# Another placement of the tiles in SBUF: the split weights 48 bytes past a multiple of 16 KB

## What is computed

```
h = rms_norm(x, ln_pre_g)
proj = einsum('bsd,de->bse', h, w_in)            # 2048 x 18432
...                                              # recurrence, attention, gates
y = einsum('bsd,de->bse', merged, w_o)
x = x + rms_norm(y, ln_post_g)
for l in range(2):
    h = rmsnorm(x, g_pre_2[l])
    u = h @ w_in_2[l]                            # 2048 x 16192
    ...                                          # three attention branches
    x = x + (gated sum of branch @ w_branch_2[l, n]) @ w_out_2[l]
```

## The kernel before

| tile | bytes | offset | over a multiple of 16 KB |
|---|---|---|---|
| raw | 16384 | 16512 | 128 |
| hl | 32768 | 32896 | 128 |
| hT, uT | 32768 each | 65664, 98432 | 128 |
| xres, mix, gat | 16384 each | 131200, 147584, 163968 | 128 |
| corr | 4096 | 180352 | 128 |
| cst, tab | 1536, 7168 | 184448, 185984 | 4224, 5760 |
| work | 32256 | 194752 | 14528 |

## Time and profile before

### The profile page before, as it was taken

One profiled execution on the slowest core, in us unless ns is written; L12 is line 12 of the kernel. 1 busy time (PEld: TensorE's weight loads), 2 busy tenths in 40 slices (PEclk: granted clock), 3 DMA queues, 4 the chain that ended last, 5 costly groups with the idle time before them and its releaser, 6 DMA issues.

```text
span 3154.9 us, 52176 instructions
## 1 busy us (share of the span) xinstructions
PE 3134.1 (99%) x18230; PEld 2741.8 (87%) x18230; DVE 2130.5 (68%) x2741; ACT 1733.0 (55%) x2291; POOL 0.2 (0%) x4
## 2 busy tenths in 40 slices
PE   9999999999999999999999999999999999999999
PEld 7888888888888788888888888888888888888888
DVE  7677575666667687766666555777776666655575
ACT  5685444444445556656555555645665656555563
POOL 0000000000000000000000000000000000000000
PEclk9999999999999999999999999999999999999999
DMA  7656655555556555565556655566556565665555
GB/s 230 194 168 200 198 187 166 183 177 172 181 167 208 178 168 163 156 198 173 174 171 192 184 181 182 181 198 186 158 157 202 170 179 167 192 189 180 178 185 175
DMA packets 569809, 571.67 MB, mean 181 GB/s; under 512 B 26352, under 2 KB 565488, under 8 KB 569712
## 3 DMA queue, kind: packets, MB, share of 16 engines
q1 hardware_dynamic: 569712, 570.42, 58.9%
HBM read 568.25 MB, written 2.10 MB: 181 GB/s over the span
## 4 chain that ended last, share of the span: by engine, by line
PE 97%; DVE 1%; ACT 1%; DMA 0%; SPq 0%; issue 0%; ACTq 0%; DVEq 0%
PE pg L537 91%; PE pa L771 1%; PE pa L788 1%; PE pa L537 1%; PE pa L778 1%; PE pa L747 1%; PE pa L789 1%; DVE hl L1276 0%; PE pa L704 0%; DMA raw<-w_o 0%; PE pa L878 0%; DMA raw<-w_in 0%; ACT hl L933 0%; SPq L456 0%; DVE uT L1357 0%
## 5 line engine op out<-in xcount | busy, mean ns | idle before, releaser
L537 PE MATMUL pg<-hT,hl 128*128 128x512 f32 x11456 | 2030.6, 337 | 1.1 <-DVE hl L1276 1.1
L537 PEld LDWEIGHTS pg<-hT,hl 128*128 128x128 f32 x11456 | 1750.9, 188 | 261.1 <-DVE hl L1276 4.2
L1276 DVE TENSOR_TENSOR hl<-raw,hl 128x1024 fp32r<-128x1024 f32 (+1 forms) x1071 | 1256.0, 1209 | 314.5 <-ACT hl L933 306.8
L933 ACT ACTIVATE hl<-raw 128x1024 fp32r<-128x1024 f32 (+1 forms) x1071 | 1084.0, 1044 | 313.1 <-PE pg L537 293.8
L537 PE MATMUL pg<-uT,hl 128*128 128x256 f32 (+1 forms) x3712 | 639.1, 333 | 15.9 <-DVE uT L1357 7.5
L537 PEld LDWEIGHTS pg<-uT,hl 128*128 128x128 f32 x3712 | 558.4, 190 | 92.2 <-issue 14.2
L941 ACT ACTIVATE corr<-pg 128x512 f32<-128x512 f32 x286 | 170.3, 596 | 843.0 <-PE pg L537 843.0
L537 PE MATMUL pg<-hl,hT 128*128 128x256 f32 (+1 forms) x1792 | 317.9, 336 | 0.0
L1283 DVE TENSOR_TENSOR work<-pg,corr 128x512 f32<-128x512 f32 (+1 forms) x154 | 105.8, 687 | 303.7 <-ACT corr L941 303.5
L537 PEld LDWEIGHTS pg<-hl,hT 128*128 128x128 f32 x1792 | 274.9, 188 | 40.7
L1283 DVE TENSOR_TENSOR gat<-pg,corr 128x512 f32 (+1 forms) x71 | 48.9, 689 | 139.4 <-ACT corr L941 139.4
(11 more groups left out here) (191 smaller groups left out, 1369.2 us busy)
## 6 DMA issues: line engine op xcount, KB each, us to landing
raw<-w_in SPq DMA_DIRECT2D x791, 512.0 KB, 4.7
raw<-w_br SPq DMA_DIRECT2D x96, 512.0 KB, 4.3
raw<-w_out SPq DMA_DIRECT2D x64, 512.0 KB, 4.7
raw<-w_rnn SPq DMA_DIRECT2D x32, 512.0 KB, 4.8
raw<-w_o SPq DMA_DIRECT2D x32, 512.0 KB, 5.0
raw<-w_att SPq DMA_DIRECT2D x16, 512.0 KB, 4.4
raw<-w_uq SPq DMA_DIRECT2D x16, 384.0 KB, 4.0
tab<-tabs SPq DMA_DIRECT2D x5, 896.0 KB, 7.2
```

The source lines that it names most:

```text
L537: return nc.tensor.matmul(out, lhsT, rhs, start=start, stop=stop, skip_group_check=True)
L933: nc.scalar.activation(hl4[:, j % 2, 0, a:a + n], raw[:, bass.ds(j % 2 * UC + a, n)], ACT.Copy)\
L1276: tt(hl4[:, j % 2, 1, a:a + n], raw[:, bass.ds(j % 2 * UC + a, n)], hl4[:, j % 2, 0, a:a + n].bitcast(F32), ALU.subtract).then_inc(lo_done, 1)
```

## The change

Only the order in which SBUF tiles are allocated and two constants change. The small tiles come first, then an unused tile `pad` of 464 columns (1856 bytes) fills up to offset 32768. `raw` starts there. `hl` gets 12 more columns (48 bytes) at its front, which `hl4` skips. The program's instructions and their order are the same on every engine; only addresses differ.

```
--- before.py
+++ after.py
@@ -56,6 +56,8 @@
 ROT_HALF = {"1": 16, "B": 8}
 
 T_C, T_S, T_R, T_M, N_TAB = 0, 256, 512, 640, 640 + 1152
+PAD = 464
+SHIFT = 12
 T_RG = T_M + 384
 
 def events(text):
@@ -200,8 +202,16 @@
         def sem(name):
             return ctx.enter_context(nc.semaphore(name))
 
+        corr = sb("corr", 2 * 512)
+        cst = sb("cst", 3 * P)
+        tab = sb("tab", N_TAB)
+        v1 = sb("v1", N_V1)
+        v2 = sb("v2", N_V2)
+        sm = sb("sm", 200)
+
+        sb("pad", PAD)
         raw = sb("raw", 2 * UC)
-        hl = sb("hl", 4 * UC, F32R)
+        hl = sb("hl", SHIFT + 4 * UC, F32R)
         hT = sb("hT", NT * 512, F32R)
         uT = sb("uT", NT * 512, F32R)
         xres = sb("xres", NT * S)
@@ -209,18 +219,12 @@
             sq_a = [mix_r[:, 5 * S * h:5 * S * h + 5 * S].rearrange("p (t n) -> p t n", n=S) for h in range(2)]
         mix = sb("mix", NT * S)
         gat = sb("gat", NT * S)
-        corr = sb("corr", 2 * 512)
-        cst = sb("cst", 3 * P)
-        tab = sb("tab", N_TAB)
-        v1 = sb("v1", N_V1)
-        v2 = sb("v2", N_V2)
-        sm = sb("sm", 200)
         work = sb("work", 31 * 256 + 128)
         pg = ctx.enter_context(nc.psum_tensor("pg", [P, 4 * 512], F32))
         pa = ctx.enter_context(nc.psum_tensor("pa", [P, 4 * 512], F32))
 
 
-        hl4 = hl[:, :].rearrange("p (s h n) -> p s h n", s=2, h=2)
+        hl4 = hl[:, SHIFT:].rearrange("p (s h n) -> p s h n", s=2, h=2)
         h3 = hT[:, :].rearrange("p (t n) -> p t n", n=512)
         u3 = uT[:, :].rearrange("p (t n) -> p t n", n=512)
         x3 = xres[:, :].rearrange("p (t n) -> p t n", n=S)
```

## The result

The changed kernel takes 3196.45 us (median of four, 3195.83 to 3196.71) where the one before takes 3156.33 us. The ratio is 1.0124, with a 95% interval of 1.0112 to 1.0137: 40 us slower. The forecast was 3156 us with 3112 to 3186 us as its range, so the time lies 10 us above the range, on the side to which 0.17 of the chances were given.

A forecast was written before the change was run, and what follows sets the result against it. TensorE's matmul rate was taken to bound the kernel. The span of 3154.9 us, four terms of 0 and 1.4 us from span to median gave 3156.3 us, with a range of 3112 to 3186 us.

The forecast's parts named there:

- What bounds the kernel: TensorE, busy 99% of the span with 17 us of waits; so its matmul rate decides the time.
- It is a fixed 13.3 ns per matmul: Each wide or narrow TensorE matmul costs 32 cycles beyond its columns, a fixed sum and not a share.
- the first term of the sum: TensorE's weight load (hl) against its moving operand (hT or uT): interval -176 us to an unknown loss, taken as 0.
- the constancy of the earlier trace: Time per matmul agreed within 0.25 ns across chunks and long stretches, so 0 was taken for TensorE's reads.
- the sign for fixedness: The excess per matmul was the same 13.3 ns in mixed stretches and in narrow ones alone, at 120.0 ns each.
- The slower one: hl's weight blocks cover nine 64-byte pieces instead of eight: four cycles more per matmul, 28 us, 3184 us; chance 0.17.
- The faster one: The 32 cycles are a collision of TensorE's two reads, ended wholly (2980 us) or a quarter (3112 us); chance 0.22.
- The third: hl lands 16, not 48, bytes from hT and uT, possibly missing any effect; same forecast, no chance of its own.
- The small terms: VectorE's split (1 us either side), ScalarE's copy, float32 matmuls and transfers into raw (0.6 us), all taken as 0.
- an unknown loss: Open upper end of the TensorE term, as no distance under 512 bytes was in the trace; 0.04 beyond 28 us.

The follow-up runs named there:

- g2: Kernel before with hl as before, hT 32 bytes further from it and uT 112 further, modulo 128; 3165.39 us.
- e3: Kernel before with hl, hT and uT moved together by 48 bytes, distances kept; 3157.59 us.
- e1: First half of the change alone on the kernel before: small tiles first and the 1856-byte pad, no 48 bytes; 3174.67 us.
- f4: As e1 but with a pad 128 bytes longer, so large tiles lie 128 over a multiple of 16 KB; 3167.92 us.
- f3: Kernel before with hl moved by 48 bytes, hT and uT by 80; 3194.08 us.
- f2: Kernel before with hl unmoved, hT and uT moved by 48 bytes; 3175.50 us.
- i1: f4 with 64 bytes put ahead of work, which then lies 64 over a multiple of 128; 3156.61 us.
- i2: Kernel before with 64 bytes put ahead of work, which then lies on a multiple of 128; 3166.29 us.
- h3: Kernel before with hl unmoved, hT 128 bytes further from it and uT 144 further; 3182.84 us.

## Why the prediction was wrong

**What bounds the kernel** was right: the rate of TensorE decides, and waits had nothing to give or take (17.1 and 16.0 us). The 13.3 ns per matmul beyond its columns is right for the kernel before as an average. "It is a fixed 13.3 ns per matmul" is not: in the same trace, in the stretch of 576, the starts give 114.9 ns behind a narrow matmul and 231.8 behind a wide one, 8.2 and 18.5 ns beyond their columns. Their mean agrees with the 13.3 ns of narrow ones alone, and the prediction took that for the proof of one fixed cost, which these two figures are not.

**The step that failed** is the first term of the sum, TensorE's weight load against its moving operand, taken at 0 "by the constancy of the earlier trace rows". The constancy was one of averages over whole stretches, and proved less than was drawn from it. All distances in that trace are multiples of 512 bytes, as the prediction itself says; the phases are equal in every one of the rows, and that is the state which the change ends. The prediction named this gap (a dependence on distances under 512 bytes) and still took 0. In place of 0 the runs showed 3.1 ns per matmul in regular stretches and 2.35 ns on average, 40 us. Even the sign for fixedness fell: narrow matmuls alone went from 120.0 to 117.4 ns (and to 113.5 in g2), so 13.3 ns is no floor.

The 32 cycles that the Trainium skill gives as the theoretical time of a fast weight load ("TensorE: Matmul & The Clock Gate", "Weight-path perf modes — Fast Weight Load (FWL) and DoubleRow") stand there for fp8, and the page doesn't name float32r. No run here shows such a load, and the cost beyond the columns doesn't stay at 32 cycles: it is 10.7 ns (117.4 - 106.7), 26 cycles, for the narrow matmuls alone in the changed kernel. The same page, "Step-by-step: what each phase is for", says that loading the next weights takes no read bandwidth from the running matmul. The runs don't agree with a reading of this by which the two reads can't disturb each other: moving the two operands' tiles against each other changes the rate, and moving them together (e3) leaves the chunk at 22.20 us.

**The trace had a hint** that was passed over. A rate that is the result of a repeating pattern also looks constant. The starts in the kernel before show such a pattern: behind narrow matmuls the intervals alternate between 112 or 113 and 117 or 118 ns. A fixed cost doesn't do that. e1 and f4 then show a second pattern at equal phases.

**The rivals.** The slower one had the sign right, but its mechanism is refuted by e3, which has the same start of `hl`, and its price (four cycles, 28 us) was too small: 7.5 cycles in regular stretches. The faster one foresaw that the cost depends on the two reads' distance, and took the kernel before for the bad case, where it was among the good ones. The third, that the change places `hl` 16 and not 48 bytes from `hT`, was true, and it was no reason for no effect: f3, at 32, and f2, at 48, are slower than before as well.

**The small terms** hold. VectorE's split stayed at 1221 ns, ScalarE's copy went from 1053 to 1055, float32 matmuls from 216.3 to 215.6 ns (3.45 us for 16). A term for `work` was missing: its move was in the table of offsets, and its phase taken up only for VectorE, ScalarE and the float32 matmuls themselves. That it can change the rate of others behind them was not thought of. It is worth 9 to 11 us in i1 and i2, at equal phases of the other tiles; in the changed kernel nothing shows it.

**The range** ended at 3186 us because the unknown loss was priced from a piece of 64 bytes that no row supports. The prediction said that the trace leaves "an unknown loss" open, and then gave only 0.04 to what lies beyond 28 us; the loss was 40.

## What to carry to other kernels

In a kernel that TensorE bounds, the offsets of the two tiles that it reads at once are a part of its speed: here placements a few bytes apart differ by 1.3%, with no instruction changed. Keep the weight tile and the moving tile at the same remainder over a large power of two (here 16 KB, distance 0), which ran the regular chunk at the best rate in every kernel tried; two multiples of 128 are not enough, as h3 shows (22.47 us for the chunk, 3182.84 for the kernel). And read the time of a wait-free stretch of matmuls whenever a tile's size or order changes, above all before an edit elsewhere is given the credit. Constancy in a trace shows only that a cost doesn't depend on what varied in it, and an average that is constant can hide costs that are not: look at the single starts before a cost is called fixed.

## What was unexpected

Addresses in steps of 16 bytes change the rate of float32r matmuls: 173.4 to 176.6 ns for one of 384 columns on average. The rule behind the table is not settled. That the two reads of TensorE meet somewhere in SBUF is consistent with all runs (only tiles that it reads were seen to matter, and `hl` and `hT` matter as a pair), but no run shows where, and neither the distance nor the sum of the phases orders the table.

The same matmuls at the same addresses have two stable rates (22.19 and 22.61 us for 128, the second worked out from 101.73 us for 576), chosen, it seems, by what ran before them. Moving a tile by 64 bytes that none of them reads moved the kernel by 9 to 11 us. Why the phase of `work` chooses stays open. So does what gave e1 another 6 us over f4 (both have equal phases, `work` included, but e1's tiles start on exact multiples of 16 KB); at least part of them lies in other stretches, such as that of 176 matmuls at about 1452 us in both. The chain of e1, then of f4:

```profile
1452.06 31.05 PE pg L541 x176
```

```profile
1451.69 30.52 PE pg L541 x176
```
